# VectorE instead of GpSimd for the low halves of 48 weight tiles, and twelve convolution steps moved into the mLSTM chunk loop

## The chip, the cores and the metric

The kernel runs on one core of a Trainium2 chip. The time is device microseconds of one execution of the whole program, and the numbers given are medians of several executions. TensorE (PE in the profile) multiplies matrices, VectorE (DVE), ScalarE (ACT) and GpSimd (POOL) compute elementwise, SyncE (SP) issues most of the DMA transfers. Each engine works through its own queue in order, and they wait for one another with semaphores.

## What is computed

Three residual blocks run one after the other on a sequence of 1024 positions and 1024 channels, all in float32. The change lies in the third block, of which this is the part that matters (an RMS norm, two branches of one projection, and a merge):

```python
h = rmsnorm_3(x, norm_g[i])
proj = h @ w_in[i]
xa, za, ub, gb, zb, gates = jnp.split(proj, split_at, axis=-1)
xc = jax.nn.silu(causal_depthwise_conv_3(xa, conv_a_w[i], conv_a_b[i]))
...                                   # q, k, v and the two gates from xc and xa
ha = mlstm_chunkwise(heads(q), heads(k) * (dh ** -0.5), heads(v), ig, lf)   # 8 chunks of 128 positions
...
ya = ((ha + skip_a[i] * xc) * jax.nn.silu(za)) @ w_proj_a[i]
ug = ub * jax.nn.sigmoid(gb)
c = causal_depthwise_conv_3(ug, conv_b_w[i], conv_b_b[i])                   # 31 taps
...
yb = (jax.nn.silu(c) * jax.nn.silu(zb)) @ w_pw2[i] + b_pw2[i]
```

## The kernel before, in words

**Products in three passes.** Activations lie channels by positions, in 8 blocks of 128 channels by 1024. A weight tile is 1024 by 128. Each float32 operand is split into a high half, rounded to the multiplier's format, and a low half, the rest; a product is hi*hi + hi*lo + lo*hi, which are the 48 matmuls of 128x512 on line 445 for a whole tile. `w_raw`, `w_hi` and `w_lo` each have two slots, used in turn. SP loads a tile into `w_raw` once the split of the tile two before it is done (semaphore `w_split`). For the 48 tiles of the list `HI_TILES` from `TAIL0` on (16 of `ug`, 8 of `za`, then 24 of `gg` and `zb` in the order of `ML_TILES`), ScalarE writes `w_hi` (`weight_hi`, line 396), once the tile has been loaded and TensorE is done with the tile two before it; `weight_lo` (line 402) subtracts it from `w_raw` and counts `w_split` up. In the kernel before GpSimd calls `weight_lo` for all 48 in a row, in its branch for "ug". TensorE starts a tile only when its `w_split` has been counted.

**What VectorE has to do there.** First `mlstm_prep_dve`: the short convolution of `xa`, then the gates' arithmetic on few partitions. Then the long convolution, in `conv_steps`: 8 channel blocks of `STEPS` = 33 steps each (a product with the gate, a first tap on line 1111, 30 taps on line 1113, and a sum over blocks), 264 steps in all, each of them one instruction on 128x1024, with a drain ahead of it. Steps 0 to 11 (`CONV_GATES` = 6, twice) stand in the gates' part, those up to `CONV_FIRST` = 148 come before `mlstm_dve`, and the other 116 are spread over the chunk loop by `CONV_SLOTS` = (6, 2, 2, 2, 3, 0), 15 in a chunk: 6 after the scores, 2, 2, 2 and 3 after the four state updates, none at the end.

**The chunk loop.** `mlstm_pe` goes through 8 chunks. Between the mLSTM's small matmuls it does 12 quarter tiles ("parts") of the projections `gg` and `zb`, so three weight tiles in a chunk. A chunk begins with eight transposes (line 1433) and the scores (line 1437), then two parts, the outputs y (lines 1448 and 1450), two parts, four state updates (line 1461) with a part behind each, transposes back (line 1467) and four parts. The outputs wait for VectorE's decayed scores (line 1535, semaphore `mx_s_ready`). The second, third and fourth update wait for VectorE's state sum before them (line 1567, semaphore `ml_cx_ready`). VectorE can deliver nothing of a chunk until it has ended the steps ahead of `mlstm_dve`.

**The order on SP.** `conv_store(k)` waits until block k of the long convolution is done, stores it and loads the operands of block k + 2; other loads stand behind it in SP's queue. The store of block 7 stands after the chunk loop in `convb_sync`, ahead of the loads of the next weight tiles (`ya`). After it SP waits for the last chunk's output and loads it back for `ya`.

## Time and profile before

| | us |
|---|---|
| median of 3 runs (lowest to highest) | 3877.3 (3874.14 to 3880.63) |
| the profiled execution | 3878.21 |
| its span | 3876.5 |
| TensorE busy | 3635.0 (94%) |
| VectorE busy | 2155.2 (56%) |
| ScalarE busy | 921.3 (24%) |
| GpSimd busy | 1151.1 (30%) |
| mean granted TensorE clock, share of full speed | 0.968 |

Busy shares are means over some ten stages with different limits. The third block's stretch of interest runs from about 2750 us to 3500 us of the span: the short convolution to 2790, the tiles of `ug` and `za` to 3050, the eight chunks to 3446, then the next stage. TensorE's row is modelled and includes overlap of neighbouring matmuls; what tells whether it waits is the idle time ahead of an instruction, in brackets in the timelines, with what ended it.

### The profile page before, as it was taken

The page shows a single profiled execution, that of the slowest core. Times are in us where ns is not written, and L with a number is a line of the kernel's source. Part 1 is how long each engine was busy: PE and PEld are TensorE (multiplying, and loading weights), DVE is VectorE, ACT ScalarE, POOL GpSimd, SP SyncE. Part 2 cuts the span into 40 slices and gives each one's busy share as a digit, 9 for nine tenths or more (in the row PEclk, how much of TensorE's full clock was granted, in tenths as well). Part 3 has the DMA queues.
Part 4 walks back from the last instruction along what each step waited for, and adds up shares of the span by engine and source line. Part 5 has one row for each costly group of instructions (what it writes and reads, how often), then busy time and mean ns, then how long its engine had stood idle before and what let it go on. Part 6 is the DMA issues. An engine that isn't in the chain of part 4 may idle for free.

```text
span 3876.5 us, 44161 instructions
## 1 busy us (share of the span) xinstructions
PE 3635.0 (94%) x17330; PEld 2976.9 (77%) x17330; DVE 2155.2 (56%) x2092; ACT 921.3 (24%) x1022; POOL 1151.1 (30%) x505
## 2 busy tenths in 40 slices
PE   7888999999999999998999999998999799989997
PEld 4677878877787887776788888876788688867775
DVE  7587541275753664545421221265389988866646
ACT  3355121121122332311210000022422122224221
POOL 0001433333243322223344444442222111123432
PEclk9899999999999999999999999998999899999998
DMA  3234213352135654633111111123434355573421
GB/s 129 67 91 130 92 44 119 111 155 65 33 125 128 169 163 125 172 101 108 44 49 49 49 45 47 51 90 97 151 119 141 119 158 158 150 236 121 140 87 60
DMA packets 538865, 415.57 MB, mean 107 GB/s; under 512 B 33352, under 2 KB 496584, under 8 KB 538720
## 3 DMA queue, kind: packets, MB, share of 16 engines
q1 hardware_dynamic: 477168, 293.94, 27.5%
q10 hardware_dynamic: 61552, 119.65, 8.2%
q8 instruction: 97, 1.59, 0.2%
q14 instruction: 48, 0.39, 0.0%
HBM read 291.00 MB, written 120.16 MB: 106 GB/s over the span
## 4 chain that ended last, share of the span: by engine, by line
PE 78%; DVE 13%; DVEq 3%; ACT 3%; DMA 2%; issue 1%; SPq 1%; ACTq 0%; POOL 0%; POOLq 0%
PE proj_ps L445 67%; DVE WORK L1113 5%; ACT stage L473 1%; DVE Hlo L592 1%; PE mix_ps L1450 1%; DVE Hlo L594 1%; PE mix_ps L696 1%; PE proj_ps L1461 1%; DVEq L552 1%; DVE AUX L675 1%; PE mix_ps L702 0%; PE mix_ps L658 0%; PE proj_ps L2069 0%; DVEq L673 0%; DVE AUX L540 0%
## 5 line engine op out<-in xcount | busy, mean ns | idle before, releaser
L445 PE MATMUL proj_ps<-Hhi,w_hi 128*128 128x512 f32 x4144 | 1331.8, 403 | 110.7 <-DVE Hlo L592 60.5
L445 PE MATMUL proj_ps<-Hlo,w_hi 128*128 128x512 f32 x4144 | 1293.3, 394 | 0.0
L445 PE MATMUL proj_ps<-Hhi,w_lo 128*128 128x512 f32 x4144 | 1288.9, 392 | 0.0
L412 POOL TENSOR_TENSOR w_hi<-w_raw,zero_col 128x1024 fp32r<-128x1024 f32 (+2 forms) x225 | 428.5, 1904 | 2094.5 <-PE proj_ps L445 1604.9
L445 PEld LDWEIGHTS proj_ps<-Hhi,w_hi 128*128 128x128 f32 x4144 | 775.1, 191 | 308.7 <-issue 76.9
L445 PEld LDWEIGHTS proj_ps<-Hlo,w_hi 128*128 128x128 f32 x4144 | 787.9, 190 | 169.2
L445 PEld LDWEIGHTS proj_ps<-Hhi,w_lo 128*128 128x128 f32 x4144 | 786.4, 190 | 169.2
L415 POOL TENSOR_TENSOR w_lo<-w_raw,w_hi 128x1024 fp32r<-128x1024 f32 (+2 forms) x225 | 583.8, 2595 | 32.0
L1113 DVE SCALAR_TENSOR_TENSOR WORK<-WORK,param_cols 128x1024 f32<-128x1024 f32 x240 | 368.6, 1536 | 19.2 <-issue 0.4
L402 POOL TENSOR_TENSOR w_lo<-w_raw,w_hi 128x1024 fp32r<-128x1024 f32 x48 | 136.6, 2846 | 548.0 <-ACT w_hi L396 548.0
L473 ACT ACTIVATE stage<-proj_ps 128x1024 f32<-128x1024 f32 x112 | 130.3, 1164 | 593.8 <-PE proj_ps L445 592.9
L530 DVE TENSOR_TENSOR XT<-XT,proj_ps 128x1024 f32<-128x1024 f32 (+1 forms) x64 | 78.0, 1219 | 328.0 <-PE proj_ps L445 328.0
L2281 DVE TENSOR_TENSOR AUX<-proj_ps,AUX 128x1024 f32<-128x1024 f32 x22 | 26.9, 1225 | 208.2 <-PE proj_ps L445 208.2
L687 ACT ACTIVATE AUX<-XT 128x1024 f32<-128x1024 f32 (+1 forms) x48 | 50.9, 1059 | 339.8 <-DVE XT L530 313.0
L445 PE MATMUL proj_ps<-AUlo,w_hi 128*128 128x512 f32 x352 | 109.7, 393 | 0.0
L445 PE MATMUL proj_ps<-AUhi,w_hi 128*128 128x512 f32 x352 | 109.1, 391 | 0.0
L445 PE MATMUL proj_ps<-AUhi,w_lo 128*128 128x512 f32 x352 | 108.7, 390 | 0.0
L486 DVE TENSOR_TENSOR stage<-proj_ps,AUX 128x1024 f32<-128x1024 f32 x24 | 29.4, 1224 | 137.1 <-PE proj_ps L445 135.0
L2270 ACT ACTIVATE AUX<-AUX 128x1024 f32<-128x1024 f32 x22 | 23.3, 1061 | 344.7 <-DVE AUX L2279 344.7
L592 DVE TENSOR_TENSOR Hlo<-WORK,Hhi 128x1024 fp32r<-128x1024 f32 x56 | 85.4, 1558 | 25.2 <-ACT Hhi L585 18.3
L540 DVE TENSOR_TENSOR AUX<-AUX 128x1024 f32<-128x1024 f32 x32 | 80.8, 2526 | 33.0 <-ACT AUX L687 32.7
L2279 DVE TENSOR_TENSOR AUX<-proj_ps,AUX 128x1024 f32<-128x1024 f32 x22 | 26.9, 1225 | 105.3 <-PE proj_ps L445 105.0
(421 smaller groups left out, 3492.8 us busy)
## 6 DMA issues: line engine op xcount, KB each, us to landing
w_raw<-in_w_in SPq DMA_DIRECT2D x101, 512.0 KB, 4.3
w_raw<-in_sgu_w_in SPq DMA_DIRECT2D x24, 512.0 KB, 3.7
w_raw<-in_w_out SPq DMA_DIRECT2D x24, 512.0 KB, 4.1
w_raw<-in_w_gate SPq DMA_DIRECT2D x22, 512.0 KB, 3.7
w_raw<-in_w_up SPq DMA_DIRECT2D x22, 512.0 KB, 3.7
w_raw<-in_s_w_in SPq DMA_DIRECT2D x16, 512.0 KB, 4.3
WORK<-mid_acs SPq DMA_DIRECT2D x8, 1024.0 KB, 16.7
mid_qkv<-stage ACTq DMA_DIRECT2D x16, 512.0 KB, 5.1
```

The costliest lines, as they stand in the source:

```text
L402: engine.tensor_tensor(wlo[slot][:, :, :], raw[slot][:, :, :], whi[slot][:, :, :].bitcast(F32), ALU.subtract)\
L412: nc.gpsimd.tensor_tensor(whi[slot][:, 0:kt, :], w, zero_col[:, 0:1].unsqueeze(2).to_broadcast([P, kt, P]), ALU.add)
L415: nc.gpsimd.tensor_tensor(wlo[slot][:, 0:kt, :], raw[slot][:, 0:kt, :], whi[slot][:, 0:kt, :].bitcast(F32), ALU.subtract).then_inc(w_split, 1)
L445: mm = nc.tensor.matmul(ps[:, h * HALF:(h + 1) * HALF], a[slot][:, k, :], b[:, at + k, h * HALF:(h + 1) * HALF], start=(k == 0 and n == 0) ...
L473: a = nc.scalar.activation(dst, src, func)
L530: nc.vector.tensor_tensor(x, x, o.unsqueeze(1), ALU.add).then_inc(psum_free, 1)
L540: nc.vector.tensor_tensor(nsq[0], nsq[0], nsq[1], ALU.add).then_inc(S("sq_added"), 1)
L552: dve.drain().then_inc(hf_ready, 1)
L592: m = nc.vector.tensor_tensor(dst, src, part.bitcast(F32), ALU.subtract)
L594: m = nc.vector.scalar_tensor_tensor(out=dst, in0=src, scalar=scale, in1=part.bitcast(F32), op0=ALU.mult, op1=ALU.subtract)
L687: nc.scalar.activation(nsq[1].unsqueeze(1), XT[:, ds(k, 1), :], ACT.Square).then_inc(S("sq_ready"), 1)
L1113: m = nc.vector.scalar_tensor_tensor(out=acc, in0=u[:, j:j + SEQ], scalar=col(f"convb_w{j}", k), in1=acc, op0=ALU.mult, op1=ALU.add)
```

## The change

GpSimd no longer makes the low halves of the 48 tiles; on GpSimd the "ug" branch is gone, and ahead of its work for `ya` it waits until all 48 are counted. VectorE makes them, at fixed places: numbers 0 and 1 in the last two blocks of the short convolution, 2 to 4 between the gates' instructions, 5 and 6 among the gates' twelve convolution steps, 7 to 24 ahead of the chunk loop with seven convolution steps between one and the next, and three in each chunk (after the scores' six steps, after the first update's step, and ahead of the wait for the chunk's copied output), the last chunk having two. `CONV_FIRST` goes from 148 to 136, and `CONV_SLOTS` to (6, 1, 2, 2, 4, 1), 16 in a chunk; the last slot stands after the next chunk's decay, so the last of the 264 steps is now the last instruction of the last chunk.

```diff
-        CONV_GATES, CONV_FIRST, CONV_SLOTS = 6, 4 * STEPS + STEPS // 2, (6, 2, 2, 2, 3, 0)
+        CONV_GATES, CONV_FIRST, CONV_SLOTS = 6, 4 * STEPS + 4, (6, 1, 2, 2, 4, 1)
...
+        def conv_first_dve(dve):
+            at = 2 * CONV_GATES + 2
+            conv_steps(dve, 2 * CONV_GATES, at)
+            tail_lo(dve, 7)
+            for m in range(8, 25):
+                conv_steps(dve, at, at + 7)
+                at += 7
+                tail_lo(dve, m)
+            conv_steps(dve, at, CONV_FIRST)
...
+        def tail_lo(dve, m):
+            weight_lo(dve, nc.vector, TAIL0 + m)
...
                 m.then_inc(S("mp_conv"), 1)
+                if k == KT - 2:
+                    dve.wait_ge(w_split, plan.p["ug"]["t0"] + 2)
+                if k >= KT - 2:
+                    tail_lo(dve, k + 2 - KT)
                 scale_x(dve, "norm_g3", k)
...
+            tail_lo(dve, 2)
             dve.wait_ge(S("gif_ready"), 1)
...
+            tail_lo(dve, 3)
             dve.wait_ge(S("xs_stored"), 16 * KT)
...
+            tail_lo(dve, 4)
             nc.vector.tensor_tensor_scan(r4(mp_m), r4(mp_lf), r4(mp_g), 0.0, ALU.add, ALU.max)
...
-                conv_steps(dve, CONV_GATES * n, CONV_GATES * (n + 1))
+                conv_steps(dve, CONV_GATES * n, CONV_GATES * n + 2)
+                tail_lo(dve, 5 + n)
+                conv_steps(dve, CONV_GATES * n + 2, CONV_GATES * (n + 1))
...
                 conv(0)
+                tail_lo(dve, 24 + 3 * c + 1)
                 dve.wait_ge(S("mx_y"), ML0["y"] + c + 1)
...
                     conv(1 + q)
+                    if q == 0:
+                        tail_lo(dve, 24 + 3 * c + 2)
+                if c + 1 < NCH:
+                    tail_lo(dve, 24 + 3 * c + 3)
                 dve.wait_ge(S("mx_copied"), ML0["copied"] + c + 1)
...
-                elif n == "ug":
-                    for m in range(TAIL0, len(HI_TILES)):
-                        weight_lo(pool, nc.gpsimd, m)
-                elif n not in ("s5_gate", "za", "gg", "zb"):
+                elif n not in ("s5_gate", "ug", "za", "gg", "zb"):
+                    if n == "ya":
+                        pool.wait_ge(w_split, plan.p["ya"]["t0"] + 2)
                     project_split(pool, n)
...
-            conv_steps(dve, 2 * CONV_GATES, CONV_FIRST)
+            conv_first_dve(dve)
```

VectorE's queue between the gates' last copy and the second block of the long convolution, before (x20 is twenty instructions in a row; line 1113 is a tap):

```order
L1272 COPY WORK<-mix_ps 128x32
L1113 SCALAR_TENSOR_TENSOR WORK<-WORK,param_cols 128x1024 x20
L1118 COPY WORK<-WORK 128x1024
L1109 TENSOR_TENSOR WORK<-WORK 128x1024
L1111 TENSOR_SCALAR WORK<-WORK,param_cols 128x1024
L1113 SCALAR_TENSOR_TENSOR WORK<-WORK,param_cols 128x1024 x30
```

The same place in the changed kernel, where the gates' copy is on line 1294:

```order
L1294 COPY WORK<-mix_ps 128x32
L1113 SCALAR_TENSOR_TENSOR WORK<-WORK,param_cols 128x1024 x2
L402 TENSOR_TENSOR w_lo<-w_raw,w_hi 128x1024
L1113 SCALAR_TENSOR_TENSOR WORK<-WORK,param_cols 128x1024 x7
L402 TENSOR_TENSOR w_lo<-w_raw,w_hi 128x1024
L1113 SCALAR_TENSOR_TENSOR WORK<-WORK,param_cols 128x1024 x7
L402 TENSOR_TENSOR w_lo<-w_raw,w_hi 128x1024
L1113 SCALAR_TENSOR_TENSOR WORK<-WORK,param_cols 128x1024 x4
L1118 COPY WORK<-WORK 128x1024
L1109 TENSOR_TENSOR WORK<-WORK 128x1024
L1111 TENSOR_SCALAR WORK<-WORK,param_cols 128x1024
L402 TENSOR_TENSOR w_lo<-w_raw,w_hi 128x1024
```

Every run of taps is now cut after seven steps by a low half of a weight tile (line 402).

VectorE's queue in a chunk from the first state sum to the chunk's output, before (line 1567 is a state sum, line 1573 the first instruction on the output):

```order
L1567 SCALAR_TENSOR_TENSOR WORK<-WORK,proj_ps 128x257 x2
L1113 SCALAR_TENSOR_TENSOR WORK<-WORK,param_cols 128x1024 x2
L1567 SCALAR_TENSOR_TENSOR WORK<-WORK,proj_ps 128x257 x2
L1113 SCALAR_TENSOR_TENSOR WORK<-WORK,param_cols 128x1024 x2
L1567 SCALAR_TENSOR_TENSOR WORK<-WORK,proj_ps 128x257 x2
L1113 SCALAR_TENSOR_TENSOR WORK<-WORK,param_cols 128x1024 x2
L1567 SCALAR_TENSOR_TENSOR WORK<-WORK,proj_ps 128x257 x2
L1113 SCALAR_TENSOR_TENSOR WORK<-WORK,param_cols 128x1024 x3
L1573 TENSOR_TENSOR WORK<-WORK 128x1024
```

The same place in the changed kernel, where the state sums are on line 1590 and the output on line 1600:

```order
L1590 SCALAR_TENSOR_TENSOR WORK<-WORK,proj_ps 128x257 x2
L1113 SCALAR_TENSOR_TENSOR WORK<-WORK,param_cols 128x1024
L402 TENSOR_TENSOR w_lo<-w_raw,w_hi 128x1024
L1590 SCALAR_TENSOR_TENSOR WORK<-WORK,proj_ps 128x257 x2
L1113 SCALAR_TENSOR_TENSOR WORK<-WORK,param_cols 128x1024 x2
L1590 SCALAR_TENSOR_TENSOR WORK<-WORK,proj_ps 128x257 x2
L1113 SCALAR_TENSOR_TENSOR WORK<-WORK,param_cols 128x1024 x2
L1590 SCALAR_TENSOR_TENSOR WORK<-WORK,proj_ps 128x257 x2
L1113 SCALAR_TENSOR_TENSOR WORK<-WORK,param_cols 128x1024 x4
L402 TENSOR_TENSOR w_lo<-w_raw,w_hi 128x1024
L1600 TENSOR_TENSOR WORK<-WORK 128x1024
```

One tap has left the place between the first two sums for a low half, one tap has been added after the last, and a second low half stands between it and the chunk's output; the third of the chunk stands after the six taps that follow the scores.

GpSimd's queue at the end of its work for this stretch, before:

```order
L410 REGISTER_ALU
L412 TENSOR_TENSOR w_hi<-w_raw,zero_col 128x1024
L415 TENSOR_TENSOR w_lo<-w_raw,w_hi 128x1024
L352 REGISTER_ALU
L352 COMPARE_AND_BRANCH
L402 TENSOR_TENSOR w_lo<-w_raw,w_hi 128x1024 x48
L352 UNCONDITIONAL_BRANCH
L352 ISA
L410 ISA
L412 TENSOR_TENSOR w_hi<-w_raw,zero_col 128x1024
L415 TENSOR_TENSOR w_lo<-w_raw,w_hi 128x1024
```

In the changed kernel:

```order
L410 REGISTER_ALU
L412 TENSOR_TENSOR w_hi<-w_raw,zero_col 128x1024
L415 TENSOR_TENSOR w_lo<-w_raw,w_hi 128x1024
L352 REGISTER_ALU
L352 COMPARE_AND_BRANCH
L352 UNCONDITIONAL_BRANCH
L352 ISA
L410 ISA
L412 TENSOR_TENSOR w_hi<-w_raw,zero_col 128x1024
L415 TENSOR_TENSOR w_lo<-w_raw,w_hi 128x1024
```

The 48 low halves have left that queue, and what it does for `ya` follows the loop of `xa` directly.

## Rows read from the trace of the kernel before

**Rows 1.** Page part 5: count, busy us and mean ns, then idle before.

```profile
L1113 DVE SCALAR_TENSOR_TENSOR WORK<-WORK,param_cols 128x1024 f32<-128x1024 f32 x240 | 368.6, 1536 | 19.2 <-issue 0.4
L402 POOL TENSOR_TENSOR w_lo<-w_raw,w_hi 128x1024 fp32r<-128x1024 f32 x48 | 136.6, 2846 | 548.0 <-ACT w_hi L396 548.0
```

**Rows 2.** Waits, 2740 to 3460: us in total, times, longest.

```profile
PE mix_ps L1448 <- DVE WORK L1535: 22.6, 1, 22.6
...
PEld proj_ps L1461 <- DVE WORK L1567: 3.5, 13, 0.5
```

**Rows 3.** Windows: length, busy PE, PEld, DVE, ACT, POOL, clock, DMA.

```profile
3057.90:3080.50 22.60, 0.06 (x1) 0.01 (x1) 21.05 (x22) 1.91 (x2) 0.00 (x0) 0.59 0.17 46
3080.50:3088.50 8.00, 7.98 (x25) 6.62 (x26) 7.57 (x6) 0.00 (x0) 0.00 (x0) 0.68 0.80 205
...
3222.00:3227.10 5.10, 5.10 (x26) 4.42 (x25) 4.84 (x4) 0.00 (x0) 0.00 (x0) 1.00 1.14 292
...
3213.91:3260.11 46.20, 45.72 (x218) 38.00 (x217) 39.72 (x51) 11.82 (x18) 7.86 (x3) 1.00 0.54 151
```

**Rows 4.** PE timeline: start us, us, instruction, idle before it.

```profile
3050.54 1.95 PE L1437 MATMUL mix_ps<-WORK 128*128 128x128 f32 x16
...
3080.52 1.20 PE L1448 MATMUL mix_ps<-WORK 128*128 128x257 f32 x2 [22.56 <-DVE WORK L1535]
...
3121.47 1.03 PE L1433 MATMUL proj_ps<-ident_sb,WORK 128*128 128x128 f32 x8
...
3240.53 1.03 PE L1461 MATMUL proj_ps<-WORK 128*128 128x257 f32 x4
...
3399.33 1.03 PE L1433 MATMUL proj_ps<-ident_sb,WORK 128*128 128x128 f32 x8
...
3452.74 1.19 PE L445 MATMUL proj_ps<-Hhi,w_hi 128*128 128x512 f32 x2 [5.01 <-DVE Hlo L592]
```

**Rows 5.** VectorE timeline ahead of the chunk loop.

```profile
2852.74 33.25 DVE L1113 SCALAR_TENSOR_TENSOR WORK<-WORK,param_cols 128x1024 f32<-128x1024 f32 x20
...
2891.34 48.62 DVE L1113 SCALAR_TENSOR_TENSOR WORK<-WORK,param_cols 128x1024 f32<-128x1024 f32 x30
...
3054.15 18.95 DVE L1113 SCALAR_TENSOR_TENSOR WORK<-WORK,param_cols 128x1024 f32<-128x1024 f32 x14
3073.48 1.77 DVE L1512 MEMSET WORK<- 128x2056 f32 x1 [0.38 <-issue]
...
3079.57 0.69 DVE L1535 SCALAR_TENSOR_TENSOR WORK<-mix_ps,WORK 128x512 f32<-128x512 f32 x1
```

**Rows 6.** GpSimd timeline, 2870 to 3100.

```profile
2877.08 2.39 POOL L402 TENSOR_TENSOR w_lo<-w_raw,w_hi 128x1024 fp32r<-128x1024 f32 x1 [7.95 <-ACT w_hi L396]
...
3040.28 3.12 POOL L402 TENSOR_TENSOR w_lo<-w_raw,w_hi 128x1024 fp32r<-128x1024 f32 x1 [8.36 <-ACT w_hi L396]
...
3096.63 2.98 POOL L402 TENSOR_TENSOR w_lo<-w_raw,w_hi 128x1024 fp32r<-128x1024 f32 x1 [43.10 <-ACT w_hi L396]
```

**Rows 7.** Line 402, low halves on VectorE elsewhere: ns min/median/max.

```profile
L402 DVE TENSOR_TENSOR w_lo<-w_raw,w_hi x16: 1160/1218/1226, 35.9 to 358.6; 128x1024 fp32r<-128x1024 f32 x16
```

**Rows 8.** VectorE timeline of the fourth chunk.

```profile
3227.46 1.43 DVE L1539 BATCH_NORM_STATS2 WORK<-mix_ps 128x6 f32<-128x256 f32 x4 [0.29 <-PE mix_ps L1450]
...
3233.83 0.88 DVE L1567 SCALAR_TENSOR_TENSOR WORK<-WORK,proj_ps 128x257 f32<-128x257 f32 x2
...
3239.10 0.88 DVE L1567 SCALAR_TENSOR_TENSOR WORK<-WORK,proj_ps 128x257 f32<-128x257 f32 x2
```

**Rows 9.** SP, VectorE and ACT timelines at the loop's end.

```profile
3429.24 1.52 SPq L382 DMA_DIRECT2D w_raw<-in_w_proj_a  x2
3444.77 13.82 SPq L606 DMA_DIRECT2D WORK<-mid_mlstm  x8
...
3437.47 2.74 DVE L1573 TENSOR_TENSOR WORK<-WORK 128x1024 f32<-128x1024 f32 x1 [5.39 <-ACT WORK L1491]
...
3441.55 0.38 ACTq L1499 DMA_DIRECT2D mid_mlstm<-WORK  x1
```


## The prediction

> **What bounds the kernel now.** I read the page's groups first and saw that GpSimd's 48 low halves and VectorE's taps lie in the same stretch, and that a tap costs 1536 ns in the mean [rows 1]. Then the list of waits of that stretch: TensorE is held by VectorE once for 22.6 us, and by small waits of 0.5 us at most, 3.5 us in 13 times [rows 2]. The timelines say where. The scores of the first chunk start at 3050.54 and two quarter tiles follow; then TensorE is idle for 22.56 us, until the decayed scores of line 1535 are there, and starts the outputs at 3080.52 [rows 4]. It was ready at 3080.52 - 22.56 = 3057.96. VectorE is never idle in that time: it works through the steps ahead of `mlstm_dve`, reaches it at 3073.48, and delivers at 3079.57 + 0.69 = 3080.26 [rows 5]. So from 2852.74 on, where the last of the gates' copies is behind VectorE, VectorE's queue is the bound until 3080, beside a TensorE that works on tiles of `ug` and `za` without a pause. In the chunks TensorE is the bound: busy 45.72 of 46.20 us, VectorE 39.72 [rows 3].
>
> **The price of a GpSimd instruction to VectorE.** Fourteen taps with no GpSimd instruction beside them (GpSimd idles for 43.10 us before 3096.63) take 18.95 us: with 1.285 us for the last one, as the others' pitch is (18.95 - 1.285)/13 = 1.36 us [rows 5, 6]. The thirty taps from 2891.34 take 48.62 us where 30 x 1.36 = 40.8 are due [rows 5]; GpSimd's low halves come every (3040.28 - 2877.08)/15 = 10.88 us [rows 6], so four of them fall in that stretch, and each costs VectorE (48.62 - 40.8)/4 = 2.0 us. On VectorE the same instruction takes 1218 ns [rows 7], some 1.30 us with its gap. Making a low half itself costs VectorE 0.7 us less than letting GpSimd do it.
>
> **Ahead of the chunk loop.** Before, 136 steps fill the 3073.48 - 2852.74 = 220.7 us, 1.62 us a step. After, 124 steps and 18 low halves (numbers 7 to 24) stand there. Without GpSimd a step is 1.36 us, and the few first taps, products and sums of each block are not longer: at most 124 x 1.36 + 18 x 1.30 = 192.0 us, so VectorE could be through at 3044.7. It can't run ahead, since number m waits for ScalarE's high half, which comes at TensorE's pace of 10.88 us a tile; seven steps and one low half are 7 x 1.36 + 1.30 = 10.82 us, just under it. Number 24 was started by GpSimd at 3040.28 [rows 6], as soon as its high half was there, so VectorE ends it at 3041.6, three steps later it is 3045.7, and from the memset to the end of line 1535 it took 3080.26 - 3073.48 = 6.8 us before [rows 5]: 3052.5, or a microsecond later where the scores themselves, which start at 3050.54 and take 1.95 us [rows 4], come last. TensorE asks at 3057.96. The wait of **22.6 us** goes whole, with some 4 us to spare. What could hold TensorE there next are the loads of the first chunk (the last rival below); SP's store of the fourth convolution block, which stands behind them in SP's queue, gets its block earlier than before.
>
> With the wait goes what follows it. The granted clock falls to 0.59 of full speed in the idle 22.6 us, and is 0.68 in the 8.0 us of outputs after it (between the levels of 1.2 and 2.4 GHz); the same outputs of the fourth chunk, at 1.00, take 5.1 us [rows 3]. That is another **2.9 us**.
>
> The low halves 0 to 6 stand among the short convolution and the gates. Each is 1.3 us where GpSimd's instruction had cost VectorE up to 2.0, or where VectorE waits anyway. Number 3 makes the gates' chain wait for a high half; TensorE has a whole tile of 10.9 us beside it. I take nothing for them, and 2 us as the upper bound.
>
> **In the chunks.** VectorE loses three GpSimd instructions, 3 x 2.0 us at most, and gains three low halves, 3.9 us, and one step, 1.36 us: from -0.7 to +1 us a chunk on 39.72 busy of 46.20 [rows 3]. It stays beside TensorE. By place: after six steps and a low half, 6 x 1.36 + 1.30 = 9.5 us, VectorE needs y. Before, the six steps with one GpSimd instruction in them took 6 x 1.36 + 2.0 = 10.2 us and it still waited 0.29 us for y [rows 8]. Between the first two sums stand now one step and one low half, 2.7 us, where two steps and a GpSimd instruction stood: the sums started 3239.10 - 3233.83 = 5.27 us apart [rows 8], of which the sum itself with gaps is 1, and will be able to start 3.6 apart. That is the sum for which TensorE's third update, at 3240.53 [rows 4], was waiting at times: it ended at 3239.98. So the 3.5 us of rows 2 go, as far as they were on the path. The starts of chunks 2 and 8 are 3399.33 - 3121.47 = 277.9 us apart, 46.31 a chunk [rows 4], against 46.20 in the one without a wait [rows 3]: 0.1 us x 8, and I take **1.2 us**, between 0 and 3.5.
>
> After the last sum stand one step and one low half more, but also no GpSimd instruction, and VectorE waits at the chunk's end for ScalarE's copies and the rows' DMA. SP loads one weight tile of each chunk some 7 us later than before, since it waits for the low half that now stands after the six steps; TensorE needs that tile over 20 us later. No price, at most 0.5 us a chunk.
>
> **The end of the loop.** Here the steps moved push something back. In the last chunk the convolution's last block was done before the last sum; now four steps follow that sum, 5.4 us, and SP's store of the block stands ahead of the two `ya` loads. They were issued at 3429.24 [rows 9] and will come 7.5 to 8 us later in this frame. GpSimd splits the first in some 10 us after issue, so at about 3447; TensorE starts `ya` at 3452.74, held by the operands' split [rows 4]. Covered by 5 us. If the cover fails, each microsecond is one of TensorE's. For the better: the first instruction on the last output took 2.74 us beside GpSimd's split [rows 9] and will take 1.2. So the output's store leaves 1.3 us sooner than 3441.55, but shares the DMA with the store and the two weight loads, and the loads for `ya` that follow at 3444.77 [rows 9] move by -1.3 to +3 us. I take **-0.6 us**.
>
> **The sum.** 22.6 + 2.9 + 1.2 + 0.6 = 27.3 us off the profiled execution's 3878.2, which gives 3850.9; that execution lies 0.9 us above the median of 3877.3. Forecast: 3850.
>
> **Rivals.** *New small waits.* Number 7 to 24 leave VectorE a spare of 0.06 us a tile, the chunk loop ties the engines more closely, and the loop's end is later on SP. If TensorE waits 1 us in each chunk for a low half or a sum, and 2 us are lost behind the loop, 10 of the 27.3 us come back: 3860. For it: the small waits of rows 2 exist already. Against it: each low half has at least 5 us between its place and TensorE's need.
>
> *The taps stay slow, and the kernel gets slower.* This is the case in which the 1536 ns are not GpSimd's doing. VectorE then comes to the loop at 2852.74 + 124 x 1.62 + 18 x 1.30 = 3077.0, 3.5 us later than now, and the wait grows. In a chunk it has a step of 1.6 and low halves of 3.9 us more, of which it can take in some 3 us; 2.5 us x 8 = 20 come on top: 3877 + 3.5 + 20 = 3900. The point from which it decides: if a step's mean falls from 1.62 by less than 0.03 us, VectorE is at the loop later than before. Against it: the slow taps come at GpSimd's pace of 10.88 us, and the fourteen without GpSimd are all fast [rows 5, 6].
>
> The Trainium skill, "SBUF — State Buffer", in the section on SBUF's two separate sides, says that VectorE, with two inputs in SBUF, and GpSimd hold a shared pair of ports exclusively for a whole instruction and that the other "fully blocks". By that rule a GpSimd instruction could cost VectorE its full length, 2.39 us where it runs unhindered [rows 6]; the taps show 2.0. With 2.4 the sum would be the same, since TensorE's pace sets when VectorE is through, but it speaks against the slow rival, which I would otherwise give twice its chance.
>
> *The wait only changes its name.* If the first chunk's rows and values, loaded over DMA, come later than VectorE now does, TensorE waits for them at 3057.96. No row here shows them landing; VectorE had no idle time before them at 3075, which bounds the price between 0 and 17 us: 3868 at worst, still faster.
>
> **How the numbers follow.** Forecast as worked out, 3846 to 3856: 0.76. New small waits, 3856 to 3866: 0.14. The changed name, 3856 to 3870: 0.04. Slow taps, near 3900: 0.04. That the gain is taken back to within noise by several of these: 0.02. The range of 3845 to 3863 takes the first whole and two thirds of the second. A difference of 0.2%, 7.8 us, is about what a measurement can tell from none. Faster by more: 0.94; within: 0.02; slower: 0.04.
>
> **What would show it.** In the profile after, taps on line 1113 of 1285 ns throughout, in mean too, with no GpSimd instruction between the loop of `xa` and `ya`; low halves on VectorE every 10.88 us, with waits of tenths for ScalarE; the memset near 3046; no idle time of TensorE ahead of the first outputs and a clock of 1.00 there; chunks 46.2 us apart; and `ya` starting some 27 us earlier. Wrong I would be where taps stay at 1.5 us, where TensorE waits for a low half, or where the first `ya` tile waits for GpSimd.

## The result

The changed kernel takes **3852.56 us** in the median of 4 runs (3850.53 to 3855.47). The kernel before, run beside it, takes 3878.88 us (3874.14 to 3880.63, 4 runs). The ratio is 0.9937, with a 95% interval of 0.9925 to 0.9950: faster by 0.63%. The forecast was 3850 with a range of 3845 to 3863. In the medians the gain is 26.3 us. The profiled execution took 3850.53 us with a span of 3848.8, which is 27.7 us less than the span of before; the prediction's sum for that difference was 27.3.

### The profile page after: what moved, and what is told of

Same layout as the page of the kernel before. It is cut to its first block, busy times and chain, and to the rows that moved or that the text cites. A ratio compares the mean times of both kernels' runs of the same rounds, so it can differ in the third digit from the quotient of the medians.

```text
span 3848.8 us, 44162 instructions
## 1 busy us (share of the span) xinstructions
PE 3626.1 (94%) x17330; PEld 2972.6 (77%) x17330; DVE 2126.0 (55%) x2140; ACT 921.1 (24%) x1022; POOL 1014.5 (26%) x457
## 4 chain that ended last, share of the span: by engine, by line
PE 83%; DVE 8%; ACT 3%; DVEq 3%; DMA 2%; issue 1%; SPq 1%; ACTq 0%; POOL 0%; POOLq 0%
PE proj_ps L445 72%; ACT stage L473 1%; DVE Hlo L592 1%; DVE Hlo L594 1%; PE mix_ps L696 1%; PE mix_ps L1472 1%; DVEq L552 1%; PE proj_ps L1483 1%; DVE AUX L675 1%; PE mix_ps L702 0%; PE proj_ps L2096 0%; PE mix_ps L658 0%; DVEq L673 0%; DVE AUX L540 0%; PE proj_ps L2097 0%
## 5 line engine op out<-in xcount | busy, mean ns | idle before, releaser
L1113 DVE SCALAR_TENSOR_TENSOR WORK<-WORK,param_cols 128x1024 f32<-128x1024 f32 x240 | 308.3, 1285 | 20.2 <-issue 0.9
L402 DVE TENSOR_TENSOR w_lo<-w_raw,w_hi 128x1024 fp32r<-128x1024 f32 x64 | 78.1, 1222 | 19.8 <-ACT w_hi L396 16.5
```

The lines of the kernel that those rows point to most:

```text
L402: engine.tensor_tensor(wlo[slot][:, :, :], raw[slot][:, :, :], whi[slot][:, :, :].bitcast(F32), ALU.subtract)\
L1113: m = nc.vector.scalar_tensor_tensor(out=acc, in0=u[:, j:j + SEQ], scalar=col(f"convb_w{j}", k), in1=acc, op0=ALU.mult, op1=ALU.add)
```

## The profile after

The first things to look at are the taps and the low halves, in part 5 of the page of the changed kernel (count, busy us and mean ns, idle before):

```profile
L1113 DVE SCALAR_TENSOR_TENSOR WORK<-WORK,param_cols 128x1024 f32<-128x1024 f32 x240 | 308.3, 1285 | 20.2 <-issue 0.9
...
L402 DVE TENSOR_TENSOR w_lo<-w_raw,w_hi 128x1024 fp32r<-128x1024 f32 x64 | 78.1, 1222 | 19.8 <-ACT w_hi L396 16.5
```

A tap takes 1285 ns in the mean where it took 1536 [rows 1], 60 us less over the 240. The 48 new low halves cost VectorE 48 x 1.22 = 59 us, so these two cancel. VectorE is still 29.2 us less busy than before (2126.0 us against 2155.2), because other instructions of it had been slow too: the eight first taps of line 1111 take 6.5 us instead of 14.2, the first instruction on a chunk's output 9.8 instead of 19.3 (eight times, in both cases). Of all that the kernel's time shows only what TensorE had waited for. The list of waits from 2740 to 3440 us no longer holds the entry of 22.6 us [rows 2], nor one of TensorE for a low half; of the 3.5 us in 13 times for a state sum it holds 0.3, in one. In their place, further down, stand waits of VectorE (us in total, times, longest):

```profile
DVE w_lo L402 <- ACT w_hi L396: 16.5, 7, 11.0
...
DVE WORK L1590 <- PE proj_ps L1483: 3.6, 7, 0.6
...
DVE WORK L1549 <- ACT WORK L1501: 3.5, 1, 3.5
```

TensorE's timeline places it (start us, us, instruction, idle before it and what ended it). Of before, one row is wanted that the sections ahead don't have, the first transposes of the loop:

```profile
3049.61 0.66 PE L1433 MATMUL proj_ps<-ident_sb,WORK 128*128 128x128 f32 x4 [1.11 <-ACT stage L473]
```

And of the changed kernel, from the same instruction (now line 1455) to the next stage:

```profile
3048.48 1.09 PE L1455 MATMUL proj_ps<-ident_sb,WORK 128*128 128x128 f32 x8 [1.11 <-ACT stage L473]
...
3056.67 0.60 PE L1470 MATMUL mix_ps<-WORK 128*128 128x257 f32 x2
...
3094.95 1.03 PE L1455 MATMUL proj_ps<-ident_sb,WORK 128*128 128x128 f32 x8
...
3372.10 1.03 PE L1455 MATMUL proj_ps<-ident_sb,WORK 128*128 128x128 f32 x8
...
3426.12 1.19 PE L445 MATMUL proj_ps<-Hhi,w_hi 128*128 128x512 f32 x2 [5.98 <-DVE Hlo L592]
...
3462.13 1.19 PE L445 MATMUL proj_ps<-Hhi,w_hi 128*128 128x512 f32 x2 [9.03 <-issue]
```

The outputs at 3056.67 have no bracket: TensorE comes from two quarter tiles and goes on. With the starts of the chunks in rows 4, the 27.7 us are divided like this:

| stretch | before | after | difference |
|---|---|---|---|
| up to the first transposes | 3049.61 | 3048.48 | -1.13 |
| first chunk | 71.86 | 46.47 | -25.39 |
| chunks 2 to 7 | 277.86 | 277.15 | -0.71 |
| last chunk and all behind it | 477.17 | 476.70 | -0.47 |
| span | 3876.5 | 3848.8 | -27.70 |

The first line is not the change's: the difference is there at 2752 us already, ahead of the first instruction that the change touches. The last line is no firmer: the same changed kernel in two other profiled executions has 473.6 and 475.8 us there. The first chunk is what a single pair of traces can tell, and it holds 25.4 of the 27.7 us: the wait of 22.56 and 2.83 more for what followed it. What belongs to the change is thus 25.4 and 0.7 us, 26.1, less what it cost behind the loop. That the whole, 27.7, came within 0.4 us of the predicted 27.3 is luck, since 1.1 us of it are not the change's. The windows of the changed kernel show that second part (length, busy PE, PEld, DVE, ACT, POOL, clock, DMA):

```profile
3056.60:3061.70 5.10, 5.10 (x26) 4.42 (x25) 4.70 (x4) 0.00 (x0) 0.00 (x0) 1.00 1.16 305
3187.32:3233.52 46.20, 45.72 (x218) 38.00 (x217) 39.88 (x55) 11.80 (x18) 0.00 (x0) 1.00 0.50 148
```

The outputs take 5.1 us at a granted clock of 1.00, the upper level of 2.4 GHz, instead of 8.0 us at 0.68 after an idle TensorE [rows 3]. The second row is a chunk without waits: VectorE is busy for 39.88 us of 46.20, against 39.72 before [rows 3].

**Where VectorE's time went.** VectorE now reaches the chunk loop 4.1 us ahead of TensorE's first transposes, where it was 23.9 us behind them. Its timeline there:

```profile
3044.34 1.77 DVE L1534 MEMSET WORK<- 128x2056 f32 x1 [0.38 <-issue]
...
3051.92 0.69 DVE L1549 TENSOR_TENSOR WORK<-WORK,tri_le_sb 128x512 f32<-128x512 f32 x1 [3.49 <-ACT WORK L1501]
...
3054.00 0.69 DVE L1557 SCALAR_TENSOR_TENSOR WORK<-mix_ps,WORK 128x512 f32<-128x512 f32 x1
```

The decayed scores (line 1557 now) are there at 3054.69, 2.0 us before TensorE asks at 3056.67. In between VectorE waited 3.49 us, for the exponential that makes the decay. ScalarE's timeline says why that was late:

```profile
3047.40 1.02 ACT L473 ACTIVATE stage<-proj_ps 128x1024 f32<-128x1024 f32 x1 [8.33 <-PE proj_ps L445]
...
3048.88 1.06 ACT L396 ACTIVATE w_hi<-w_raw 128x1024 fp32r<-128x1024 f32 x1 [0.46 <-ACT stage L473]
3049.96 1.28 ACT L1501 ACT_TABLE_LOAD   x1
3051.25 0.63 ACT L1501 ACTIVATE WORK<-WORK 128x512 f32<-128x512 f32 x1
```

In ScalarE's queue the exponential stands behind the last tile of `za`, which comes out of TensorE at 3047.4, behind a high half, and behind a load of the function table of 1.28 us. TensorE's pace sets when that chain begins. So VectorE can't deliver sooner however early it reaches the loop, and the spare of 2.0 us is what this place has.

## Experiments

Kernels that ran together on one chip shared the runs of the kernel before. Its medians were 3879.61 us (E1 to E4), 3877.24 (E5 to E7 and a repeat of the changed kernel) and 3873.64 (E8 and a second repeat), so ratios are compared, or kernels of one group.

### E1: the low halves on VectorE, all convolution steps where they were

```diff
-        CONV_GATES, CONV_FIRST, CONV_SLOTS = 6, 4 * STEPS + 4, (6, 1, 2, 2, 4, 1)
+        CONV_GATES, CONV_FIRST, CONV_SLOTS = 6, 4 * STEPS + STEPS // 2, (6, 2, 2, 2, 3, 0)
```

(The changed kernel with the step table of before.)

> The changed kernel with CONV_FIRST back at 148 and the slots back at (6, 2, 2, 2, 3, 0): only the low halves move to VectorE. The theory: VectorE's steps ahead of the loop cost 1.36 us without GpSimd beside them, so it reaches the loop 12 x 1.36 = 16.3 us later than the changed kernel's 3044.3, at 3060.7, and has the decayed scores 6.8 us later, at 3067.5. TensorE asks at 3056.7, so it waits 10.8 us, and up to 2 us of slower clock follow; some 1.5 us come back at the end of the loop, where the last block of the long convolution is done earlier: 3862 to 3867, a gain of 12 to 17 us of the 26. A rival, by which the gain is all in the order of the steps and the exchange of engines is worth nothing: within 4 us of the kernel before.

Measured: 3864.25 us in the median of 8 runs, ratio 0.9966 [0.9954, 0.9978]. From E1's page, and from its timelines of VectorE and TensorE:

```profile
L1113 DVE SCALAR_TENSOR_TENSOR WORK<-WORK,param_cols 128x1024 f32<-128x1024 f32 x240 | 308.3, 1285 | 20.2 <-issue 1.3
```

```profile
3061.09 1.77 DVE L1534 MEMSET WORK<- 128x2056 f32 x1 [0.38 <-issue]
```

```profile
3068.13 1.20 PE L1470 MATMUL mix_ps<-WORK 128*128 128x257 f32 x2 [11.21 <-DVE WORK L1557]
...
3109.34 0.93 PE L1455 MATMUL proj_ps<-ident_sb,WORK 128*128 128x128 f32 x7
```

The taps are at 1285 ns with the low halves alone moved, and VectorE arrives 12.5 us behind the first transposes (3048.57 in this trace) instead of 23.9. TensorE's wait is halved, to 11.21 us. This makes the low halves' change the cause of the fast taps and of 11.35 us of the wait, and shows that it does not do the whole.

### E2: the steps moved, the low halves left on GpSimd

```diff
-        CONV_GATES, CONV_FIRST, CONV_SLOTS = 6, 4 * STEPS + STEPS // 2, (6, 2, 2, 2, 3, 0)
+        CONV_GATES, CONV_FIRST, CONV_SLOTS = 6, 4 * STEPS + 4, (6, 1, 2, 2, 4, 1)
```

(The kernel before with the step table of after.)

> The kernel before with CONV_FIRST 136 and the slots (6, 1, 2, 2, 4, 1): only the twelve steps move, GpSimd keeps the low halves. The theory: 12 x 1.62 = 19.4 us off the 3073.5 at which VectorE reached the loop, so 3054.0 and the decayed scores at 3060.8 against TensorE's 3058.0: a wait of 3 us instead of 22.6, and a little clock. In the chunks one step more beside GpSimd's three instructions, up to 1 us a chunk of it seen by TensorE: 3855 to 3864. So most of the gain would be had by either order, and the two parts don't add. The rival, by which VectorE is short of time in the chunks as soon as it has 16 steps and GpSimd's instructions to bear: 3865 to 3875.

Measured: 3861.48 us (4 runs), ratio 0.9958 [0.9941, 0.9974]. E2's VectorE and TensorE:

```profile
3061.34 1.77 DVE L1512 MEMSET WORK<- 128x2056 f32 x1 [0.38 <-issue]
```

```profile
3053.78 1.09 PE L1433 MATMUL proj_ps<-ident_sb,WORK 128*128 128x128 f32 x8 [1.11 <-ACT stage L473]
...
3068.37 1.20 PE L1448 MATMUL mix_ps<-WORK 128*128 128x257 f32 x2 [6.25 <-DVE WORK L1535]
...
3108.69 1.03 PE L1433 MATMUL proj_ps<-ident_sb,WORK 128*128 128x128 f32 x8
```

This execution reached the loop 4.17 us later than that of before (3053.78 against 3049.61), so positions are read from the first transposes: VectorE arrives 7.56 us behind them, 16.3 us sooner than before. That is 12 steps of 1.36 us, the price of a step with no GpSimd instruction beside it. I had priced the twelve at the mean of the stretch, 1.62 us each, or 19.4. But the steps that went are in effect the last ones ahead of the loop, and those ran beside an idle GpSimd already [rows 5, 6].

**The two parts don't add up, and the trace says by how much.** VectorE's arrival moves by 11.35 us in E1 and 16.31 in E2, 27.66 together; in the changed kernel it moves by 28.0 (from 23.87 behind the transposes to 4.14 ahead). The arrivals add. TensorE had only 22.56 us of wait to give; the other 5.5 us are the 2.0 us of spare and the 3.49 us for which VectorE itself waits for ScalarE. In the times: 15.4 us less in E1, 18.1 in E2, 33.5 together, against 26.3 for the whole change. Either part alone brings six to seven tenths of the gain.

Chunks 2 to 7 take 277.35 us in E1 and 277.36 in E2, 46.20 to 46.24 each, against 277.86 before and 277.15 after. Neither has an entry for a state sum in its list of waits. So the small waits of the chunks [rows 2] go with either part: they were there only with two steps and a GpSimd instruction together between the first two sums.

### E3: the chunk loop's low halves back on GpSimd

```diff
-                tail_lo(dve, 24 + 3 * c + 1)
...
-                    if q == 0:
-                        tail_lo(dve, 24 + 3 * c + 2)
-                if c + 1 < NCH:
-                    tail_lo(dve, 24 + 3 * c + 3)
...
-                        pool.wait_ge(w_split, plan.p["ya"]["t0"] + 2)
+                        pool.wait_ge(w_split, plan.p["gg"]["t0"] + 3)
+                        for m in range(TAIL0 + 25, len(HI_TILES)):
+                            weight_lo(pool, nc.gpsimd, m)
```

> The changed kernel, but with the low halves of the chunk loop (numbers 25 to 47) made by GpSimd again, as in the kernel before, and those ahead of it by VectorE. The theory: the wait ahead of the first outputs stays gone, since it hung on numbers 7 to 24; in each chunk VectorE bears three GpSimd instructions of 2.0 us instead of three low halves of 1.3, and TensorE's small waits come back: 0.1 to 0.3 us a chunk, 1 to 2.5 us, so 3853 to 3856. The rival, by which the gain in the chunks is larger than the 0.7 us seen in the two traces because 16 steps and GpSimd don't fit beside TensorE: 3858 or more.

Measured: 3853.22 us (4 runs, 3843.94 to 3855.88), ratio 0.9931 [0.9910, 0.9952], which the runs can't tell from the changed kernel's 0.9937. A window of one chunk in E3, and its 23 low halves on the page:

```profile
3187.32:3233.52 46.20, 45.71 (x217) 38.00 (x216) 39.01 (x52) 11.82 (x18) 8.35 (x3) 1.00 0.53 148
```

```profile
L402 POOL TENSOR_TENSOR w_lo<-w_raw,w_hi 128x1024 fp32r<-128x1024 f32 x23 | 62.0, 2698 | 596.0 <-ACT w_hi L396 596.0
```

With GpSimd in the chunk VectorE is busy for 39.01 us, with the low halves its own for 39.88; either way TensorE's 46.20 us set the chunk. Half of the change, 23 of the 48 low halves, buys nothing that can be measured. The gain is made by the low halves ahead of the loop and by the steps.

### E4: a GpSimd instruction that reads SBUF, added to the changed kernel

Each high half from number 3 on lets GpSimd subtract one block of `XT` from another into an unused part of `WORK`; nobody waits for the result.

```diff
                     if n == "ya":
+                        pool.wait_ge(w_split, plan.p["ug"]["t0"] + 5)
+                        for m in range(TAIL0 + 3, len(HI_TILES)):
+                            pool.drain()
+                            pool.wait_ge(S("w_hi_ready"), m + 1)
+                            nc.gpsimd.tensor_tensor(WORK[:, 18 * SEQ:], XT[:, 0, :], XT[:, 1, :], ALU.subtract)
                         pool.wait_ge(w_split, plan.p["ya"]["t0"] + 2)
```

> The changed kernel with 45 added GpSimd instructions, one for each high half from number 3 on: a subtraction of two blocks of x in SBUF, 128x1024, into a free part of WORK, whose result nobody reads; it is the same form of instruction as the low half that GpSimd made before, at the same times. The theory (a GpSimd instruction costs VectorE 2.0 us wherever it reads): seven steps and a low half take 10.8 + 2.0 = 12.8 us against TensorE's 10.9 a tile; after four tiles of slack TensorE waits for low halves, 1.9 us a tile for some 13 tiles, then some 5 us ahead of the first outputs, and 1 to 3 us in each chunk: 3885 to 3910, slower than the kernel before, with taps of 3.3 us once a tile. The rival (the taps were slow because GpSimd and the others worked on the same weight buffers, not because it worked at all): no change from 3852.

Measured: 3891.52 us in a single run, 39 us above the changed kernel and 12 above the kernel before. VectorE, then GpSimd, then TensorE in E4:

```profile
2984.84 11.43 DVE L1113 SCALAR_TENSOR_TENSOR WORK<-WORK,param_cols 128x1024 f32<-128x1024 f32 x7
```

```profile
2985.99 2.39 POOL L2802 TENSOR_TENSOR WORK<-XT 128x1024 f32<-128x1024 f32 x1 [10.26 <-ACT w_hi L396]
```

```profile
3022.29 0.73 PE L445 MATMUL proj_ps<-Hhi,w_hi 128*128 128x512 f32 x2 [1.02 <-DVE w_lo L402]
...
3034.93 0.73 PE L445 MATMUL proj_ps<-Hhi,w_hi 128*128 128x512 f32 x2 [1.44 <-DVE w_lo L402]
...
3047.61 0.73 PE L445 MATMUL proj_ps<-Hhi,w_hi 128*128 128x512 f32 x2 [1.49 <-DVE w_lo L402]
```

The seven taps between two low halves take 11.43 us, with 9.45 in E5 below: 1.98 us for one instruction of 2.39 us, the 2.0 that the prediction had worked out. And from 2972 us on TensorE waits at each of eight tiles for its low half, 11.3 us in all: tiles start 12.6 to 12.7 us apart (once 12.2) instead of 10.88. Seven steps and a low half are 10.82 us by the prediction's estimate, 0.06 under TensorE's tile; with 2 us more VectorE is the bound, and since the low halves stand in its queue, TensorE goes at VectorE's pace. E4's span is 41.0 us longer than that of the changed kernel, and 24 of them lie ahead of the loop, 7.8 in the first chunk (54.26 us, with a wait of 4.87 for the scores), 5.3 in chunks 2 to 7 and 3.8 behind. This is the price of fixed places: they work only while nothing disturbs VectorE.

### E5: GpSimd instructions that only write, at the same places

```diff
+                            nc.gpsimd.memset(WORK[:, 18 * SEQ:], 0.0)
+                            pool.drain()
+                            nc.gpsimd.memset(WORK[:, 18 * SEQ:], 0.0)
```

(In place of the `tensor_tensor` of E4: 90 of them, 954 to 955 ns in the median, one of them 1407.)

> The changed kernel with 90 added GpSimd instructions, two memsets of 128x1024 in a row into a free part of WORK for each high half from number 3 on: GpSimd instructions at the same times as in e4, which only write SBUF and read nothing there. It tells which GpSimd instruction costs VectorE its 2 us. If any does, VectorE loses time at every tile and the kernel takes 3870 to 3900. If only one that reads SBUF does, as the Trainium skill, 'SBUF - State Buffer', says of VectorE instructions with two inputs there, the taps stay at 1285 ns and only tensor_scalar and copies may be held: 3852 to 3856. I hold the second for likelier, 0.6.

Measured: 3855.71 us in a single run; the changed kernel had 3855.36 in the same group. E5's list for line 1113 (ns min/median/max) and for line 1111, the first taps, and then VectorE and GpSimd:

```profile
L1113 DVE SCALAR_TENSOR_TENSOR WORK<-WORK,param_cols x240: 1283/1284/1289, 2834.8 to 3411.4; 128x1024 f32<-128x1024 f32 x120
```

```profile
L1111 DVE TENSOR_SCALAR WORK<-WORK,param_cols x8: 812/814/1402, 2832.4 to 3332.7; 128x1024 f32<-128x1024 f32 x8
```

```profile
2999.66 9.45 DVE L1113 SCALAR_TENSOR_TENSOR WORK<-WORK,param_cols 128x1024 f32<-128x1024 f32 x7
```

```profile
2999.43 0.96 POOL L2804 MEMSET WORK<- 128x1024 f32 x1
```

No tap of the 240 is longer than 1289 ns, with a GpSimd memset beside many of them, as at 2999.66. So it is not GpSimd's being at work that holds the taps, nor its writes, but an instruction of it that reads SBUF (SBUF is the memory on the chip in which these tensors lie). All those seen here read two operands; a GpSimd instruction that reads one was not tried. The one-input instruction of line 1111 is touched by the memset, at the most 1402 ns instead of 814. The Trainium skill, "SBUF — State Buffer", in the section on SBUF's two separate sides, has it so: an exclusive lock on shared ports, for VectorE instructions with two SBUF inputs only against a GpSimd instruction that reads SBUF, and for those in a two-port mode against any. The first half agrees with E4 and E5, except that a tap lost 1.98 us to an instruction of 2.39. The second fits the 1402 ns of line 1111 if that instruction is in such a mode, which no run here shows.

### E6: the first `ya` loads ahead of the last convolution store

```diff
             conv_store(sp, 6)
-            conv_store(sp, 7)
             for m in range(2):
                 load_tile(sp, "ya", 0, m)
+            conv_store(sp, 7)
```

> The changed kernel with SP's two weight loads for ya ahead of the store of the last block of the long convolution, instead of behind it. The change had put these three transfers beside the store of the last chunk's output (its landing took 5.7 us instead of 3.2). The theory: with the weight loads gone from there, the output lands 1 to 2 us sooner, and what follows with it: 1 to 2 us faster than the changed kernel, 3850 to 3852 where that is 3852.6. The rival: the loads behind are bound by their own bytes, no difference.

Measured: 3853.82 us (5 runs), ratio 0.9941 [0.9927, 0.9956]; the changed kernel in the same group 3855.36, 0.9942 [0.9928, 0.9956]. That is no difference that the runs can tell. The loop's end in the changed kernel, VectorE, SP and ScalarE:

```profile
3404.50 5.36 DVE L1113 SCALAR_TENSOR_TENSOR WORK<-WORK,param_cols 128x1024 f32<-128x1024 f32 x4
3410.03 1.23 DVE L1600 TENSOR_TENSOR WORK<-WORK 128x1024 f32<-128x1024 f32 x1 [0.16 <-ACT WORK L1513]
```

```profile
3409.89 0.33 SPq L1141 DMA_DIRECT2D mid_convb<-WORK  x1
3410.27 1.52 SPq L382 DMA_DIRECT2D w_raw<-in_w_proj_a  x2
3418.28 13.85 SPq L606 DMA_DIRECT2D WORK<-mid_mlstm  x8
```

```profile
3412.59 0.38 ACTq L1521 DMA_DIRECT2D mid_mlstm<-WORK  x1
```

and in E6, VectorE and GpSimd:

```profile
3400.56 8.81 DVE L1113 SCALAR_TENSOR_TENSOR WORK<-WORK,param_cols 128x1024 f32<-128x1024 f32 x4
```

```profile
3402.30 2.65 POOL L412 TENSOR_TENSOR w_hi<-w_raw,zero_col 128x1024 fp32r<-128x1024 f32 x1 [667.95 <-PE proj_ps L445]
3405.09 3.19 POOL L415 TENSOR_TENSOR w_lo<-w_raw,w_hi 128x1024 fp32r<-128x1024 f32 x1
```

In the changed kernel the last output's store leaves beside three other transfers of 512 KB and lands after 5.7 us, where it took 3.2 before. With the loads issued first, as in E6, it lands after 3.2 us. But then GpSimd splits the first `ya` tile beside the last four taps, which take 8.81 us instead of 5.36, and the store is issued 43.9 us after the chunk's start instead of 40.5. What the output's sooner landing gives, the slower taps take. The order that the change brought about, with the loads behind the steps, has the merit of keeping GpSimd's split away from the taps.

### E7 and E8: the loads of the third and fourth `ya` tile ahead of the merge's operands

The third `ya` tile is the largest wait left here: TensorE stands idle for 9.03 us ahead of 3462.13, where it was 4.29 before (the tile itself starts only 1.4 us later, counted from the last chunk's start, since before TensorE waited 2.89 us more among the first tiles). Its weights are queued on SP behind 6 MB of operands that are wanted later.

```diff
+            for m in range(2, 4):
+                load_tile(sp, "ya", m // 2, m % 2)
             sp.dma_start(cn_c, tiles_of("convb")).then_inc(S("cn_in"), 16)
             wait_stored(sp, "zb")
             sp.dma_start(cn_z[:, 0:4, :], tiles_of("zb")[:, 0:4, :]).then_inc(S("cn_z_in"), 16)
-            for m in range(2, 4):
-                load_tile(sp, "ya", m // 2, m % 2)
```

E7 is this on top of E6:

> e6 with the loads of the third and fourth ya tile ahead of the 4 MB of the convolution's result instead of behind it and 2 MB more. TensorE was idle 9.0 us ahead of its third ya tile in the changed kernel, 4.3 us in the one before. The theory: that wait goes, but 1 MB ahead of the convolution's data delays it by some 3 us, and the next stage (yb) hangs on VectorE's work on that data, so at most a few us are gained: 3846 to 3854. The rival, by which only VectorE's chain counts: up to 3 us slower than e6.

Measured: 3849.80 us (6 runs), ratio 0.9927 [0.9913, 0.9941], 5.6 us under the changed kernel of the same group. E8 is this alone:

> The changed kernel with only the second edit of e7: the loads of the third and fourth ya tile ahead of the 4 MB of the convolution's result, the two first ya loads back behind the last store. In e6 and e7 GpSimd's split of the first ya tile fell beside the last four taps, which took 8.8 us instead of 5.4, and the last output left 3.4 us later. Without that the next stage should begin as in the changed kernel and the wait of 9 us for the third ya tile should still go: 3 to 6 us faster than the changed kernel beside it, and up to 2 us faster than e7. The rival, by which the order of these loads only moves the wait to the convolution's data: no faster than the changed kernel.

Measured: 3847.18 us (3840.78 to 3849.24, 5 runs), ratio 0.9926 [0.9912, 0.9939]. It ran beside the changed kernel again:

> The changed kernel, beside e8 on the same chip: 3850 to 3856.

which took 3852.61 us (3850.23 to 3854.45, 5 runs), ratio 0.9944 [0.9931, 0.9958]. E8's slowest run is below the other's fastest, and the difference is 5.4 us. SP and TensorE in E8 (the last line is the first tile of the next projection):

```profile
3434.53 1.06 SPq L382 DMA_DIRECT2D w_raw<-in_w_proj_a  x2
3435.63 2.96 SPq L1628 DMA_DIRECT2D WORK<-mid_convb  x1
```

```profile
3486.70 3.57 PE L1659 MATMUL mix_ps<-ones,WORK 128*128 128x1 f32 x16 [4.14 <-DVE WORK L1723]
...
3532.66 0.70 PE L445 MATMUL proj_ps<-Hhi,w_hi 128*128 128x512 f32 x2 [0.82 <-DVE Hlo L592]
```

The wait of 9.03 us has no successor at the third tile, and with it goes a slow clock behind it (0.69 for 7.9 us in the changed kernel). Part of the gain is given back at line 1659, where TensorE now waits 4.14 us, instead of 0.21, for VectorE's part of the merge, whose operands come later. Counted from the last chunk's start (3374.47 in E8), the last line above stands at 158.2 us; in the three profiled executions of the changed kernel it is 164.4, 163.2 and 163.4. So 5.0 to 6.2 us are left, and the medians say 5.4. E8 beats both kernels.

The first repeat of the changed kernel, beside E5 to E7, has only to say how far one kernel's executions differ:

> The changed kernel itself, beside e6 and e7 on the same chip: 3850 to 3855, ratio to the kernel before 0.993.

Measured: 3855.36 us (5 runs). Its loop starts at 3057.25, 8.8 us later than the 3048.48 of the first profiled execution, with equal code ahead; its first chunk is 46.45 us. Places upstream and downstream vary by several us; the pitch of the chunks varies by hundredths.

## Why the prediction was right, step by step

**The wait, 22.6 us: right, whole.** It went, and no other took its place. Its inner steps: VectorE's arrival was forecast at 3045.7 and is 3044.34, in an execution that was 1.1 us early. The price of a GpSimd instruction, 2.0 us, is 1.98 in E4. TensorE waited for none of the 48 low halves.

**The spare, some 4 us: mis-sized, it is 2.0.** The step that failed is "from the memset to the end of line 1535 it took 6.8 us before". It took 10.35 us (3044.34 to 3054.69). I had carried over a duration that was measured when VectorE came last; when it comes first, the exponential on ScalarE is the last thing to be ready. I had allowed one microsecond for TensorE's scores and had not looked at ScalarE's queue, where that chain stands behind the last `za` tile. It cost nothing here. In an edit that counted on 4 us it would have.

**The clock, 2.9 us: right,** 2.83 measured as what the first chunk gained beside the wait. The runs show that it hangs little on how long TensorE idles: over the changed kernel's first chunk of 46.47 us, E1 has 60.77, of which 11.21 are the wait and 3.1 the rest, and E2 has 54.91, with 6.25 and 2.2.

**The chunks, 1.2 us: right in kind, 0.7 in size.** I took 0.1 us from each of eight; six of them lie between two starts that the trace gives, and they gave 0.12 each. The first chunk's share can't be told from the clock's. The reason was wider than the prediction's: by E1 and E2 either part would do. VectorE's sums start 4.13 us apart rather than 5.27 [rows 8], not the forecast 3.6, because it now waits 0.58 us for TensorE there. The fourth chunk of the changed kernel:

```profile
3207.25 0.88 DVE L1590 SCALAR_TENSOR_TENSOR WORK<-WORK,proj_ps 128x257 f32<-128x257 f32 x2
...
3211.38 0.87 DVE L1590 SCALAR_TENSOR_TENSOR WORK<-WORK,proj_ps 128x257 f32<-128x257 f32 x2 [0.58 <-PE proj_ps L1483]
```

**The loop's end, -0.6 us: wrong in sign, by 1 to 4 us.** Read from the last chunk's start, the output's store leaves at 40.49 instead of 42.22 us, 1.7 sooner (forecast 1.3), and line 1600 takes 1.23 us instead of 2.74 [rows 9]. But it lands after 5.7 us instead of 3.2, so the loads for `ya` are issued at 46.2 instead of 45.4; the first tile starts at 54.0 instead of 53.4, and the third at 90.0 instead of 88.7. The other two executions of the changed kernel have 55.6 and 54.8 for the first tile and 91.1 and 91.6 for the third. That the moved steps do it shows in E1, which leaves them and has 53.1 and 89.0, and in E2, which moves them and has 55.6 and 90.2; these are single traces. The output's loads move by 0.7 to 2.0 us, in the bounds of -1.3 to +3 given for them; of the two effects that I named, the shared DMA was the larger. The `ya` weights came 8.3 us later instead of 7.5 to 8, but it is still the operands that the first tile waits for. I had also looked no further than the first tile, and the third has the larger wait. The total of the last stretch, -0.47 us, hides it, since it varies more than that from one execution to the next.

**The low halves 0 to 6, nothing: right.** Number 3 waits 2.58 us for its high half, and the copy behind it comes 2.8 us later than before (with the 1.1 us by which this execution is early taken out). But VectorE then waits for TensorE, 3.50 us where it was 4.48, and the eight short scans behind that start at the same place in both. They are shorter themselves, below.

**The rivals.** The slow taps are refuted by E1 alone: 1285 ns, at most 1289. New small waits did not come (one weight load waits 0.3 us for a state sum), and E4 shows what they would have been: 2 us more for VectorE in a tile, and the whole stretch goes at its pace. The wait did not change its name.

## What to carry to other kernels

Before moving work off an engine that has time to spare, look at what it costs its neighbour: here a GpSimd instruction of 2.4 us cost VectorE 2.0 us, and VectorE did the work itself in 1.3. Gains from two edits on one wait add in the arrival of the engine that is late, but not in time: they end where the next engine's queue begins, so look at that queue, and don't carry over a duration that was measured while another engine was last. And when a stretch is quick because side work has fixed places in a queue, its margin (by estimate 0.06 us a tile here) is what a later edit will break.

## What the runs showed of the hardware

- What GpSimd does to VectorE depends on both instructions. Beside a GpSimd `tensor_tensor` that reads SBUF (2.39 us) a tap with two SBUF inputs loses 1.98 us; beside a memset (0.96 us) it loses nothing, while a one-input instruction of 814 ns became 1402 (E4, E5).
- It holds for work on four partitions too: the eight scans of 4x128 that took 4.78 us before, with a low half of GpSimd started at 2820.12 beside them, take 2.62 us after. The same eight scans before and after:

```profile
2819.66 4.78 DVE L1257 TENSOR_TENSOR_SCAN WORK<-ones,WORK 4x128 f32<-4x128 f32 x8
```

```profile
2818.53 2.62 DVE L1276 TENSOR_TENSOR_SCAN WORK<-ones,WORK 4x128 f32<-4x128 f32 x8
```

- What the first chunk lost beside a wait of TensorE itself was 2.2, 3.1 and 2.8 us for waits of 6.25, 11.21 and 22.56 us. The granted clock behind them was 0.60 for 5.6 us, 0.50 for 5.9 and 0.68 for 8.0, and then back at 0.97 to 1.00. A short wait before small matmuls thus costs, in proportion, the most: at 6.25 us a third comes on top.
- One store of 512 KB lands after 3.2 us with little beside it and after 5.7 to 7.0 us beside three others of its size (the changed kernel, E2, E3 and E8).
